# Loading x of an encoder by four transfers of 128 rows in place of eight of 64

## What is computed

```python
def reference(x, ...):
    for i in range(DEPTH):                       # DEPTH = 2
        hn = _rmsnorm(x, norm_mix[i])
        if mixer == 0:
            y = _pool_mixer(hn, a_w_in[slot], a_w_group[slot], a_scale[slot], a_w_out[slot])
        ...
        x = x + y
        hn = _rmsnorm(x, norm_ffn[i])
        ...
        x = x + y
    return _rmsnorm(x, norm_final)
```

## Time and profile before

| | us |
|---|---|
| median of three executions | 1533.2 (1531.36 to 1534.36) |
| span of the profiled execution | 1531.6 |
| PE busy in it | 1487.0 (97%) |
| DVE busy | 1166.2 (76%) |
| ACT busy | 996.8 (65%) |
| moved by DMA | 468.31 MB |

### The profile page before, as it was taken

The page is one execution under the profiler, slowest core; times in us unless marked ns, Lnnn a source line. Parts: engine busy times, 40 slices in busy tenths (PEclk is TensorE's granted clock), DMA queues, the critical chain, the costliest instruction groups (busy, mean ns, idle before and its releaser), DMA issues.

```text
span 1531.6 us, 19275 instructions
## 1 busy us (share of the span) xinstructions
PE 1487.0 (97%) x7570; PEld 1216.4 (79%) x7570; DVE 1166.2 (76%) x1009; ACT 996.8 (65%) x861; POOL 151.5 (10%) x130
## 2 busy tenths in 40 slices
PE   8999999999989999999999999999999999999995
PEld 6888888899979987788777788777888777887783
DVE  5555445455455455999899988899898999898996
ACT  5443434343363446777798777888776888776994
POOL 0000000013034022400000300000300002000000
PEclk9999999999999999999999999999999999999998
DMA  9655555566507642699999999999999999999994
GB/s 335 210 192 167 191 175 182 192 194 219 189 32 221 219 165 83 227 410 407 362 408 422 399 409 411 386 411 418 401 414 404 385 411 417 403 402 406 386 394 167
DMA packets 151119, 468.31 MB, mean 306 GB/s; under 512 B 9792, under 2 KB 15936, under 8 KB 138480
## 3 DMA queue, kind: packets, MB, share of 16 engines
q1 hardware_dynamic: 144720, 453.93, 78.8%
q0 software_dynamic: 2816, 9.96, 2.3%
q10 hardware_dynamic: 3488, 3.13, 0.7%
HBM read 459.62 MB, written 7.37 MB: 305 GB/s over the span
## 4 chain that ended last, share of the span: by engine, by line
PE 77%; DVE 15%; ACT 3%; issue 2%; DMA 1%; SPq 1%; DVEq 0%; ACTq 0%
DVE wlo L405 10%; PE bS L424 6%; PE bS L423 6%; PE bS L425 6%; PE bY L423 6%; PE bY L424 6%; PE bY L425 6%; PE bG L423 4%; PE bU L423 4%; PE bU L424 4%; PE bU L425 4%; PE bG L424 4%; PE bG L425 4%; ACT whi L399 2%; DVE wlo_more L405 2%
## 5 line engine op out<-in xcount | busy, mean ns | idle before, releaser
L405 DVE TENSOR_TENSOR wlo<-raw,whi 128x2048 fp32r<-128x2048 f32 x368 | 834.8, 2295 | 187.3 <-ACT whi L399 186.5
L399 ACT ACTIVATE whi<-raw 128x2048 fp32r<-128x2048 f32 x368 | 699.6, 1914 | 262.3 <-PE bS L425 136.3
L405 DVE TENSOR_TENSOR wlo_more<-raw_more,whi 128x2048 fp32r<-128x2048 f32 x58 | 131.8, 2286 | 9.8 <-ACT whi L399 9.6
L399 ACT ACTIVATE whi<-raw_more 128x2048 fp32r<-128x2048 f32 x58 | 110.3, 1915 | 21.9 <-PE bS L425 9.1
L1010 PE MATMUL bY<-whi,hTh 128*128 128x512 f32 x224 | 91.4, 408 | 7.8 <-DVE wlo L405 5.2
L423 PE MATMUL bY<-whi,hTh 128*128 128x512 f32 x224 | 89.7, 401 | 0.0
L424 PE MATMUL bY<-whi,hTl 128*128 128x512 f32 x224 | 88.9, 397 | 0.0
L553 POOL TENSOR_TENSOR bias<-biasrev,band 128x256 f32<-128x256 f32 x32 | 33.2, 1038 | 510.5 <-DMA biasrev<-toeplitz 381.8
L1010 PE MATMUL bS<-whi,eTh 128*128 128x512 f32 x192 | 76.2, 397 | 0.0
L423 PE MATMUL bS<-whi,eTh 128*128 128x512 f32 x192 | 76.2, 397 | 0.0
L424 PE MATMUL bS<-whi,eTl 128*128 128x512 f32 x192 | 76.1, 396 | 0.0
(11 more groups left out here) (476 smaller groups left out, 3376.3 us busy)
## 6 DMA issues: line engine op xcount, KB each, us to landing
raw<-in_m_w_gate_up_dram SPq DMA_DIRECT2D x188, 1024.0 KB, 13.8
raw<-in_m_w_down_dram SPq DMA_DIRECT2D x90, 1024.0 KB, 13.7
raw<-in_b_w_in_dram SPq DMA_DIRECT2D x36, 1024.0 KB, 5.1
raw_more<-in_m_w_gate_up_dram SPq DMA_DIRECT2D x36, 1024.0 KB, 15.0
raw<-in_f_w_gate_up_dram SPq DMA_DIRECT2D x28, 1024.0 KB, 5.1
raw_more<-in_m_w_down_dram SPq DMA_DIRECT2D x22, 1024.0 KB, 13.5
raw<-in_f_w_down_dram SPq DMA_DIRECT2D x14, 1024.0 KB, 5.0
raw<-in_a_w_out_dram SPq DMA_DIRECT2D x4, 1024.0 KB, 16.0
```

Of the source, the lines that this page charges most:

```text
L399: nc.scalar.activation(whi[:, h], raw_of(r), ACT.Copy).then_inc(hi_done, 1)
L405: nc.vector.tensor_tensor(wlo_of(r), raw_of(r), whi[:, h].bitcast(F32), ALU.subtract).then_inc(lo_done, 1)
```

## The change

`load_x` takes a block `tb` in place of `a`. One transfer now brings the 128 tokens of a block and a half of the columns, 256 KB, and lands in all 128 partitions. The source is written with the dimensions a (2 steps of one token), m (64 steps of four tokens) and the 512 columns, in this order from the outside; the destination has 128 partitions. Each place where an engine waits for x waits for 32 in place of 64. SP issues one transfer of the first half and two of the second, ACT one of the first.

```diff
-        def load_x(engine, a, kh):
+        def load_x(engine, tb, kh):
             sl = slice(kh * 512, kh * 512 + 512)
-            engine.dma_start(x[a % 2 * 64:a % 2 * 64 + 64, a // 2, sl],
-                             x_in[0].rearrange("(m a) d -> a m d", a=4)[a][:, sl]).then_inc(x_in_done[kh], 16)
+            engine.dma_start(x[:, tb, sl], x_in[0].rearrange("(m t a) d -> t a m d", t=NT, a=2)[tb][:, :, sl]
+                             ).then_inc(x_in_done[kh], 16)
...
-            for a in range(3):
-                load_x(sp, a, 0)
+            load_x(sp, 0, 0)
             for b in range(4):
                 sp.dma_start(raw[:, 0, b * 512:b * 512 + 512],
                              tile_source(0)[b * P:b * P + P, :]).then_inc(first_full[b], 16)
-            for a in range(4):
-                load_x(sp, a, 1)
+            for tb in range(NT):
+                load_x(sp, tb, 1)
...
-                    pe.wait_ge(x_in_done[kh], 64)
+                    pe.wait_ge(x_in_done[kh], 32)
...
-            load_x(act, 3, 0)
+            load_x(act, 1, 0)
```

More of the change, by code:

```diff
@@ L1125, in root @@
                 if n == 0:
-                    act.wait_ge(x_in_done[0], 64)
-                act.wait_ge(*((x_in_done[1], 64) if n == 0 else (x_final, 1) if n == 4 else (x_sum, (2, 4, 8)[n - 1])))
+                    act.wait_ge(x_in_done[0], 32)
+                act.wait_ge(*((x_in_done[1], 32) if n == 0 else (x_final, 1) if n == 4 else (x_sum, (2, 4, 8)[n - 1])))
                 nc.scalar.activation((hn, squares)[n >= 3][:, 1], x[:, 1], ACT.Square, accum_out=ss[:, 1:2]).then_inc(sq_done, 1)
@@ L1549, in _ @@
             make_lo(dve, 2)
-            dve.wait_ge(x_in_done[0], 64)
-            dve.wait_ge(x_in_done[1], 64)
+            dve.wait_ge(x_in_done[0], 32)
+            dve.wait_ge(x_in_done[1], 32)
             stats(0)
```

## The result

The changed kernel takes 1551.87 us (median of four, 1551.54 to 1552.58); the kernel before took 1532.28 beside it. The ratio is 1.0127, with a 95% interval of 1.0113 to 1.0141: 19.6 us slower. The forecast was 1550.0, in a range of 1543 to 1558. The spans of the profiled executions, 1550.8 and 1531.6, differ by 19.2.

What follows compares the result with a forecast made beforehand. PE, busy 97% of the span, was taken as the bound, so a start delay shifts everything: tile 1's landing 15.2 us later plus 1.6 for the clock, 16.8 on 1533.2, gives 1550.0 us, range 1543 to 1558.

Steps and rivals of the forecast that it cites:

- What bounds the start: At the start: PE, busy 97%, never makes up delays; tile 1's landing at 14.83 us leads its first matmul by 5.86.
- Fewer issues: On SP's queue: four issues go, tile 1 is issued some 2.4 us earlier, gaining 0.33 us at most.
- The form of the transfer: In x's loads: the source's outermost 2 confines each transfer to two of 16 DMA engines; chance 0.80.
- The landing: Tile 1, behind 661 KB per engine at 24.3 KB per us, lands at 30.0 us, 15.2 later (13.0 to 18.6).
- The lag of 1 us to the landing: In DMA transfers: about 1 us passes from the last byte to the landing, beyond the transfer itself.
- The clock: On PE behind the gap ahead of tile 1: a stretch at 1.2 GHz costs 0 to 1.6 us, taken as 1.6.
- All 16 engines: Rival for x's loads: all 16 engines, or at least 8, share each transfer; gain 0.33 us, 1532.9; chance 0.12.
- x's rows slow in themselves at 13.3 KB per us: Rival for x's loads on two engines: tile 1 lands at 47.8, 33 us later, time 1567.8; chance 0.04.
- A lone engine at 30: Rival for x's loads: two engines at 30 KB per us, tile 1 10.0 us later, no half clock, 1543.2; chance 0.04.

Runs made afterwards that it cites:

- the exchanged form: The changed kernel with x's source as [64, 2, 512] in place of [2, 64, 512], each token in the same partition: 1531.1 us, ratio 0.9992.
- the experiment with tile 1 ahead: The changed kernel with tile 1 issued ahead of x's second half on SP's queue: 1551.63 us, ratio 1.0120.
- The fillers: The changed kernel with nine more matmuls of zeros between PE's end of tile 0 and its wait for tile 1: 1550.28 us, ratio 1.0113.
- the split old transfers: The kernel before, its eight transfers of 64 rows with the source written as [2, 32, 512] in place of [64, 512]: 1552.61 us, ratio 1.0129.
- with eight: The changed kernel with the source of each transfer of x as [8, 16, 512]: 1537.81 us, ratio 1.0034.
- with four: The changed kernel with the source of each transfer of x as [4, 32, 512]: 1543.0 us, ratio 1.0074.

## Why the prediction was right, point by point

**What bounds the start: right.** The chain behind tile 1's landing is 5.86 us in both traces, and the whole delay of 19.12 us is still there at 448 us. The 97% of PE meant what it was read to mean.

**Fewer issues: right in size.** With the transfers on all engines, the ratio is 0.9992, and 1 lies in its interval. The sum for the single execution was off, however: 1.80 us gained there, where 0.33 was the limit. I had taken PE as the next late one, ending tile 0 at 20.37. That end held a stretch at half clock (13.5 to 16.6), and in the execution of the exchanged form the clock stayed at 1.00 there; PE was ready earlier, and tile 1, landing 1.72 us earlier, set the start.

**The form of the transfer: right.** A share of 0.13 from 8 to 18 us is two engines of 16, and one of 0.26 with an outermost 4 is four; exchanging the source's dimensions takes the loss away, and writing the old transfers with an outermost 2 brings it. The rule that the prediction cites from the Trainium skill ("DMA: Bandwidth & Descriptors", the section on why a DMA increments its semaphore by 16: the largest number of engines up to 16 that divides the slowest dimension of both sides) agrees with the shares for 2 and 4 (0.13 and 0.26), and the cost that falls from 4 to 8 goes its way. The row on disjoint partition halves among the rules for kernel authors of the same page of the Trainium skill, that one transfer over 128 partitions is to be preferred, did not hold for the changed kernel, 19.6 us slower; with the source's dimensions exchanged the ratio is 0.9992, which can't be told from 1.

**The landing: 17.7 in place of 15.2, inside the bounds 13.0 to 18.6.** The mis-sized term is the rate of an engine. 24.3 KB per us was taken throughout, from a stretch with no x in it. The two engines ran at 25.5 alone, and slower while the others were busy: x's second half, 262 KB for each, took from 16.78 to 29.99, 13.2 us where the sum had 10.8 (16.5 to 27.3). The first 1.8 of these passed alone at 25.5, so about 216 KB took 11.4 us, some 19 KB per us (an estimate from these numbers). I had waved aside the slow stretch of the earlier trace rows at 8 us as that of many engines against one another, which two would not cause; they were not alone, so it came back.

**Smaller steps.** x's first half came at 16.78 and not at 13.8. I had left tile 0's four pieces out of the queue ahead of it; with them it is 1.8 + 333 / 24.3 + 1 = 16.5. And SP was stuck earlier than I said, 8.02 us at x itself, so that tile 1 was issued at 12.28; it cost nothing, as the experiment with tile 1 ahead shows. The lag of 1 us to the landing was read low: the first transfer's own numbers give 0.71 + 2.9 - 1.8 - 0.3 = 1.5.

**The clock: 1.6 forecast, 1.44 measured.** The size came out, but not the way to it: the gap ahead of tile 1 was to be about 4 us and was 2.20, since turning x's second half and ending tile 0 took PE 6.2 us (29.99 to 36.17, half clock in most of it) in place of some 4. That a gap of half the length cost as much is in part luck. The fillers show that the gap ahead of tile 1 has to do with it. Its length alone does not decide: with x's second half alone in the new form, PE idled 2.76 us there and the clock stayed at 1.00 behind it, where 2.20 us in the changed kernel were followed by 0.50. Longer gaps (2.95 us in the split old transfers, 3.87 with eight, 4.62 with four) were each followed by a stretch at 0.50. What decides stays open.

**Rivals.** All 16 engines: refuted by the share of 0.13. x's rows slow in themselves at 13.3 KB per us: refuted, 25.5 alone. A lone engine at 30: refuted by the same number.

## What to carry to other kernels

Before two transfers are joined into one, write down the dimensions of both sides from the outside in: a small outermost dimension of the source, even one that only reorders rows, put the whole transfer on that many DMA engines here. A small one on the destination's side was not tried. The price is not only that transfer's own: each later transfer of the same queue is also split over all engines and ends only when the loaded ones have come to it. A share of DMA engines that sits at 2/16 or 4/16 while the kernel waits for data is how it looks in a profile.

## What the runs showed of the hardware that I had not expected

A DMA engine moved 25.5 KB per us in rows of 2 KB with 14 others idle, and 17.9 with all at work while x was under way (287 GB/s together), though 16 engines reach 389 GB/s on the weights. The form of x's transfers seems to matter for this too. With x on all 16 engines and tiles of weights beside it, the windows of before (64 partitions at a time) and then of the exchanged form (128 partitions) read

```profile
8.00:10.00 2.00, 2.00 (x14) 1.57 (x12) 0.65 (x2) 1.52 (x4) 0.00 (x0) 1.00 1.09 236
```

```profile
4.00:6.00 2.00, 2.00 (x6) 1.60 (x5) 0.00 (x0) 0.00 (x0) 0.00 (x0) 1.00 0.97 343
8.00:10.00 2.00, 2.00 (x15) 1.74 (x14) 0.26 (x1) 1.13 (x4) 0.00 (x0) 1.00 1.03 389
```

Engines that were as busy moved 236 GB/s in the one and up to 389 in the other. It can't be the 64 partitions alone: with an outermost 8, each transfer of x landed in 128 partitions, and 16 busy engines were as slow:

```profile
10.00:12.00 2.00, 2.00 (x14) 1.66 (x12) 0.56 (x2) 1.43 (x4) 0.00 (x0) 1.00 1.08 219
```

What does slow them was not tried by itself. The last surprise is SP: one issue lasted 8.02 us, from 4.22 to 12.24, and in the last four of them 14 of the 16 engines had nothing to do. So work piled up on two engines is enough to hold up the issue of transfers for all.
